# Two transformer blocks on one core: the output product by halves, its norm weights as a row, and chunk 3 of each such product one token later

## The chip, the cores and the metric

The kernel runs on one core of one Trainium2 chip. The time is that of one execution on the device, in microseconds (us); less is better. Three runs of the kernel before gave 1738.46, 1740.90 and 1743.47, median 1740.9.

## What is computed

Two transformer blocks on 512 tokens of 1024 features, in float32. The change touches four places of the same kind: a product of all tokens with a weight matrix, an RMS norm of its rows, a sum onto the residual h, and the RMS norm of h that begins the next stage. Cut to these:

```
mixed = concat(rmsnorm(y_conv), rmsnorm(y_att))
h = h + rmsnorm(mixed @ w_out, norm_mix_post)        # "out", then "hx"
hn = rmsnorm(h, norm_x_pre)
qx = hn @ w_q_x                                      # "qx"
kx, vx = split(rmsnorm(mem, norm_mem) @ w_kv_x)      # "kx", "vx": from mem, not from h
ox = softmax(qx kx^T / 16) vx
h = h + rmsnorm(ox @ w_o_x, norm_x_post)             # "ox", then "hf"
hn = rmsnorm(h, norm_ffn_pre)
h = h + rmsnorm((silu(g) * up) @ w_down, norm_ffn_post)   # "down0..2", then "h2"
# second block: ... h = h + merged @ w_out_2 ("out2", then "h4"), and a last MLP onto h
rmsnorm(x, g) = x / sqrt(mean(x^2) + eps) * g        # over the 1024 features of a token
```

## The kernel before, in words

**Products in three parts.** Each float32 operand is split into a high part (cast to float32r) and a low part (the rest); a product is high x high, high x low and low x high, all summed in one PSUM bank. Weights come in chunks of 1 MB: SyncE (SP) loads a chunk into one of three raw buffers, ScalarE casts it to w_high (`high`, L930, the cast at L945), GpSimd (POOL) subtracts it into w_low in four parts of 512 columns (`low_parts`, L783, at L801). w_high and w_low have a ring of two; a chunk in HOMES (L59) has buffers of its own in the arena (L372) and waits for no chunk of the ring. A raw buffer is loaded anew when the chunk three before has its low part; SP goes through the plan (make_plan) in order, so whatever waits in `before` (L627) holds the loads behind it.

**Groups by rows.** `rows` (L126) makes a group like out, vx, ox, down and out2: two halves of 512 output columns, each in two chunks of (mostly) 512 rows of the weights. So chunks 0 and 1 give the first half, chunks 2 and 3 the second, each for four tiles of 128 tokens (for vx two tiles, of mem). `product` (L2292) of one chunk and one token tile is 12 matmuls of 512 columns, eight with w_high (L2325, L2326), then four with w_low (L2329), each of which waits for its part of w_low. I write 2.1 for chunk 2 and token tile 1. down2 has 6 row blocks, so its chunks 1 and 3 are half as long. Groups by columns (gu, qx, up) are T mode, L2334 to L2338; where a stage does them in pieces between others (L2246 to L2248), a piece is three matmuls.

**Norm and turn.** The next product needs h normed, scaled and transposed. `stat` (L947) is the sum of squares and the root on ScalarE. `xn` (L1493) is the scaling on VectorE into stage: for the phases in NATURAL (L60) by the root and a row of norm weights that was loaded into all partitions (L1503), for the others by the root alone (L1508). `turn` (L2225, the transposes at L2222) lets TensorE turn the eight blocks of one token tile into two banks. For the phases in DIRECT ScalarE then casts the bank to xT_high (L965) and VectorE subtracts to xT_low (`lows`, L1510, at L1517). For the others VectorE first multiplies by the norm weights as a column (L1534), ScalarE casts that (L968) and VectorE subtracts (L1541).

**The four places before.** ox, down2 and out2 are done by `by_token` (L2250) on TensorE: chunks 0 and 1 for all tokens, then 2.0, 3.0, 2.1, 3.1, 2.2, turn 0, 3.2, 2.3, turn 1, 3.3, and turns 2 and 3 among the first products of the next stage (`first_tiles`, L2264). On ScalarE and VectorE, ox and down2 have `post_halves` (L1127, L1848): the first half's squares are summed and its norm weights multiplied in while TensorE does the second half; then, for each token, square, root, sum onto h (L1880), sum of squares of h, scaling.

out is different. TensorE does its four chunks one after another for all tokens, then vx's four chunks for two tiles each, with turn 0 to turn 2 of hx behind chunks 1 to 3 of vx, and turn 3 behind it (L2532 to L2547). ScalarE (`post`, L1168) copies every tile to ynat, takes the sum of squares over 1024 columns, and VectorE (`post`, L1790, and `staggered`, L1800) scales, adds to h and scales again, by the column way. Then the first 16 pieces of qx (chunk 0), which need all tokens of hx (`low_all`), and the cross-attention, which does the other pieces between its own steps.

## Time and profile before

| | |
|---|---|
| median of three runs | 1740.9 us |
| the profiled execution: time, span | 1742.11 us, 1740.4 us |
| busy TensorE, GpSimd, ScalarE, VectorE | 96%, 42%, 38%, 36% |
| mean granted clock of TensorE | 0.986 |
| out chunk 0 begins; chunk 2; vx; qx; cross-attention | 304.3; 330.8; 352.5; 393.2; 407.0 us |
| down2's and out2's turn 0 | 914.2; 1368.6 us |

The span is that of one execution, taken by the hardware profiler; the time is measured around it. A line of the timeline gives the start, the length, the engine, the line of the kernel, the operation with what it writes and reads, and in brackets how long the engine had been idle and whose work released it. "PEclk" is the share of TensorE's full clock that was granted. Matmuls are pipelined, so each record overlaps the next: one of 512 columns is 0.39 us long and starts 0.23 us after the one before. In records that merge several (x4), the length is of the group.

### The profile page before, as it was taken

The numbers are of one execution on the slowest core, as the hardware profiler recorded it, in microseconds if no ns is written. First come the engines' busy times: TensorE is split into PE (matmuls) and PEld (weight loads), VectorE is DVE, ScalarE is ACT, GpSimd is POOL, SyncE is SP. The second block draws the span as 40 slices with busy tenths as digits, with TensorE's granted clock in tenths as the row PEclk, the third lists the DMA queues.
The fourth block names the chain that finished last, engine by engine and source line by source line (L and its number), as shares of the span: only waits on it lengthen the run. The fifth ranks groups of instructions, "written<-read, shape, count | busy, mean of one in ns | idle before, by whom it ended". The sixth has DMA issues, their size and how long they took to land. (4 is left out here: it accounts for less than half of the span.)

```text
span 1740.4 us, 22686 instructions
## 1 busy us (share of the span) xinstructions
PE 1666.9 (96%) x8699; PEld 1325.8 (76%) x8699; DVE 632.5 (36%) x1169; ACT 666.8 (38%) x1005; POOL 733.4 (42%) x639
## 2 busy tenths in 40 slices
PE   7989899979999999999998999999999999999999
PEld 5767668757668888878877787767778888888887
DVE  6432765272324111101137534454556331213131
ACT  4223567363344233231235534443554431313140
POOL 5223334463143443454443544323454354444443
PEclk9999899999999999999999999999999999999999
DMA  5243202232131433343231234222254323232321
GB/s 175 75 145 83 72 26 74 85 132 70 41 96 43 127 97 97 97 143 92 71 108 49 93 101 140 77 83 84 74 200 151 97 73 97 97 97 97 97 98 49
DMA packets 152876, 165.55 MB, mean 95 GB/s; under 512 B 11981, under 2 KB 114496, under 8 KB 152768
## 3 DMA queue, kind: packets, MB, share of 16 engines
q1 hardware_dynamic: 145152, 150.69, 27.1%
q10 hardware_dynamic: 7616, 13.41, 2.2%
q8 instruction: 69, 1.13, 0.3%
q14 instruction: 39, 0.32, 0.1%
HBM read 155.17 MB, written 9.30 MB: 94 GB/s over the span
## 5 line engine op out<-in xcount | busy, mean ns | idle before, releaser
L801 POOL TENSOR_TENSOR w_low<-raw,w_high 128x512 fp32r<-128x512 f32 x505 | 671.5, 1362 | 888.2 <-ACT w_high L945 887.8
L945 ACT CAST w_high<-raw 128x2048 fp32r<-128x2048 f32 (+1 forms) x128 | 241.2, 1884 | 255.6 <-PE bank L2329 242.3
L2334 PE MATMUL bank<-xT_high,w_high 128*128 128x512 f32 (+1 forms) x672 | 249.2, 376 | 0.0
L2335 PE MATMUL bank<-xT_low,w_high 128*128 128x512 f32 (+1 forms) x672 | 248.8, 375 | 0.0
L2325 PE MATMUL bank<-w_high,hid_high 128*128 128x512 f32 x432 | 172.0, 398 | 0.3 <-ACT w_high L945 0.3
L2326 PE MATMUL bank<-w_high,hid_low 128*128 128x512 f32 x432 | 171.8, 398 | 0.0
L2338 PE MATMUL bank<-xT_high,w_low 128*128 128x512 f32 (+1 forms) x672 | 156.6, 375 | 0.7 <-POOL w_low L801 0.7
L2246 PE MATMUL bank<-xT_high,w_high 128*128 128x512 f32 (+1 forms) x360 | 152.4, 423 | 3.7 <-DVE xT_low L1541 3.2
L2335 PEld LDWEIGHTS bank<-xT_low,w_high 128*128 128x128 f32 x672 | 127.3, 189 | 22.4
L2334 PEld LDWEIGHTS bank<-xT_high,w_high 128*128 128x128 f32 x672 | 127.2, 189 | 22.4
L2248 PE MATMUL bank<-xT_high,w_low 128*128 128x512 f32 (+1 forms) x360 | 142.6, 396 | 0.0
L2247 PE MATMUL bank<-xT_low,w_high 128*128 128x512 f32 (+1 forms) x360 | 142.0, 394 | 0.0
L2338 PEld LDWEIGHTS bank<-xT_high,w_low 128*128 128x128 f32 x672 | 121.0, 189 | 23.6 <-POOL w_low L801 1.3
L2329 PE MATMUL bank<-w_low,hid_high 128*128 128x512 f32 x432 | 120.4, 399 | 1.7 <-POOL w_low L801 1.7
L2325 PE MATMUL bank<-w_high,xT_high 128*128 128x512 f32 x256 | 102.3, 400 | 3.5 <-DVE xT_low L1541 3.5
L2326 PE MATMUL bank<-w_high,xT_low 128*128 128x512 f32 x256 | 100.8, 394 | 0.0
L2329 PEld LDWEIGHTS bank<-w_low,hid_high 128*128 128x128 f32 x432 | 82.0, 190 | 22.3 <-POOL w_low L801 2.4
L2325 PEld LDWEIGHTS bank<-w_high,hid_high 128*128 128x128 f32 x432 | 81.6, 189 | 20.4 <-ACT w_high L945 0.7
L2326 PEld LDWEIGHTS bank<-w_high,hid_low 128*128 128x128 f32 x432 | 81.7, 189 | 19.8
L2198 DVE TENSOR_TENSOR h<-h,bank 128x512 f32<-128x512 f32 x40 | 27.5, 688 | 172.9 <-PE bank L2329 172.8
L2246 PEld LDWEIGHTS bank<-xT_high,w_high 128*128 128x128 f32 (+1 forms) x360 | 67.9, 189 | 27.8 <-issue 9.0
L1902 DVE TENSOR_TENSOR qbuf<-silu,bank 128x512 f32<-128x512 f32 x22 | 15.1, 688 | 187.8 <-PE bank L2338 187.8
(427 smaller groups left out, 2542.9 us busy)
## 6 DMA issues: line engine op xcount, KB each, us to landing
raw<-in_w_in SPq DMA_DIRECT2D x33, 1024.0 KB, 5.0
raw<-in_w_down SPq DMA_DIRECT2D x26, 1024.0 KB, 5.0
raw<-in_w_gate_up SPq DMA_DIRECT2D x44, 512.0 KB, 5.0
raw<-in_w_up SPq DMA_DIRECT2D x16, 1024.0 KB, 5.2
raw<-in_w_kv_x SPq DMA_DIRECT2D x8, 1024.0 KB, 5.2
raw<-in_w_out SPq DMA_DIRECT2D x8, 1024.0 KB, 5.0
gate_dram<-qbuf ACTq DMA_DIRECT2D x20, 256.0 KB, 2.0
sg<-gate_dram ACTq DMA_DIRECT2D x6, 768.0 KB, 5.3
```

Source lines behind the costliest of these rows:

```text
L801: ins = pool.tensor_tensor(low[:, cs], full[:, cs], high[:, cs], ALU.subtract)
L945: own.tell(act.copy(split_slot(c, wh), split_slot(c, raw)), wh_done)
L2198: own.tell(dve.tensor_tensor(y, y, src[:, :], ALU.add), dense_v)
L2246: pe.matmul(ps, ah, bh, start=first, stop=False)
L2247: pe.matmul(ps, ah, bl, start=False, stop=False)
L2248: return pe.matmul(ps, al, bh, start=False, stop=last)
L2325: pe.matmul(ps[:, :], xh[:, k, js], ch[:, q, :], start=first and q == 0, stop=False)
L2326: pe.matmul(ps[:, :], xl[:, k, js], ch[:, q, :], start=False, stop=False)
L2329: mm = pe.matmul(ps[:, :], xh[:, k, js], cl[:, q, :], start=False, stop=last and q == len(ks) - 1)
L2334: pe.matmul(ps[:, t0:t1], ch[:, k, cs], xh[:, k, t0:t1], start=q == 0, stop=False)
L2335: pe.matmul(ps[:, t0:t1], ch[:, k, cs], xl[:, k, t0:t1], start=False, stop=False)
L2338: mm = pe.matmul(ps[:, t0:t1], cl[:, k, cs], xh[:, k, t0:t1], start=False, stop=q == len(ks) - 1)
```

## The change

- Chunks 2 and 3 of out are done by token, as in by_token, with turns 0 and 1 of hx inside; vx follows, product by product, with turn 2 behind its first and turn 3 behind its third; the other five stand between turn 3 and qx.
- out and hx take the way of ox and hf: post_halves on ScalarE and VectorE, norm_x_pre as a row (hx in NATURAL), no copy of the tiles to ynat by ScalarE, no column product. The old `post` and `staggered` go.
- vx's first chunk gets a home of its own, at 16448 and 24640 of the arena, where the attention's probabilities were.
- SP loads norm_mix_post and norm_x_pre ahead of out's chunk 3; before, norm_mix_post stood ahead of vx. norm_ffn_pre goes into the same row as norm_x_pre, so its load waits for hx's last scaling.
- ScalarE casts vx's chunk 1 ahead of the last square of out and chunk 2 ahead of hx's last copies; its copies of vx's tiles come after all of hx.
- In all four places (out, ox, down2, out2) the order is now 2.0, 2.1, 3.0, 3.1, 2.2, turn 0, and on as before.

post_halves of VectorE is moved up unchanged; it is shown once, where it is added.

```diff
@@ -56,8 +56,8 @@
 
 HEAD_GAINS = (("g_na_q_2", ND), ("g_na_k_2", ND), ("g_mem_q_2", MD), ("g_mem_k_2", MD))
 GAIN_LOADS = sum(P // d for _, d in HEAD_GAINS)
-HOMES = {"gu0": 0, "if": 0, "up0": 1}
-NATURAL = ("hf", "h2", "h4")
+HOMES = {"gu0": 0, "if": 0, "up0": 1, "vx": 2}
+NATURAL = ("hx", "hf", "h2", "h4")
 DIRECT = NATURAL + ("hm", "hna")
 
 
@@ -164,7 +164,7 @@
     p.columns("xin", w_in, [1024, 1280], readers="V")
     p.columns("kx", a["w_kv_x"], [0, 256, 512, 768])
     p.use(0, 1, 2, 3)
-    p.rows("out", a["w_out"], 0, 2, 4)
+    p.rows("out", a["w_out"], 0, 2, 4, readers="V")
     p.use(0, 1)
     p.rows("vx", a["w_kv_x"], 1024, 2, 2, readers="X")
     p.columns("qx", a["w_q_x"], [0, 256, 512, 768])
@@ -370,7 +370,8 @@
         rtmp = at("rtmp", o, [P, 2, S])
         gnat = [at("gain_natural", 49216, [P, D]), shared[:, 0:D]]
         homes = [(at("home_high_0", 61504, [P, CW], F32R), at("home_low_0", 69696, [P, CW], F32R)),
-                 (at("home_high_1", 8192, [P, CW], F32R), at("home_low_1", 24576, [P, CW], F32R))]
+                 (at("home_high_1", 8192, [P, CW], F32R), at("home_low_1", 24576, [P, CW], F32R)),
+                 (at("home_high_2", 16448, [P, CW], F32R), at("home_low_2", 24640, [P, CW], F32R))]
         hidh, hidl = at("hid_high", 0, [P, 8, S], F32R), at("hid_low", 16384, [P, 8, S], F32R)
 
...
@@ -629,8 +630,8 @@
                 "kv": lambda: (vector_loads(), position_loads()),
                 "kcvc": lambda: small_loads(),
                 "kx": lambda: (late_mem(), bias_windows()),
-                "vx": lambda: post_gain("norm_mix_post", o_taken, 2 * ST),
-                "ox": lambda: (post_gain("norm_x_post", h_ready, 4), natural_gain(0, "norm_ffn_pre", pv_done, 2 * ST * PER_GROUP)),
+                "ox": lambda: (post_gain("norm_x_post", h_ready, 4),
+                               natural_gain(0, "norm_ffn_pre", xn_ready, ntile["hx", 3] + 1)),
                 "down0": lambda: second_memory(),
                 "gu2": lambda: (post_gain("norm_ffn_post", h_ready, 8),
                                 natural_gain(0, "g_mix_2", xn_ready, ntile["hf", 3] + 1)),
@@ -710,6 +711,9 @@
                         x_load(j)
                 if c is c.group.chunks[0] and c.group.name in before:
                     before[c.group.name]()
+                if c is G["out"].chunks[3]:
+                    post_gain("norm_mix_post", o_taken, 2 * ST)
+                    natural_gain(0, "norm_x_pre", pv_done, 2 * ST * PER_GROUP)
                 if c.group.name == "gate2":
                     i = c.group.chunks.index(c)
                     for hd in beside.get(i, ()):
@@ -889,8 +893,7 @@
             low_parts(len(plan.chunks))
 
         STATS = [("x", j) for j in range(4)] + [("mem", j) for j in range(2)] + [("att", j) for j in ATT_ORDER]
-        STATS += [("yo", 0), ("yo", 1), ("hx", 0), ("yo", 2), ("hx", 1), ("yo", 3), ("hx", 2), ("hx", 3)]
-        for ph, nx in (("yx", "hf"), ("yf", "h2")):
+        for ph, nx in (("yo", "hx"), ("yx", "hf"), ("yf", "h2")):
             if ph == "yf":
                 STATS += [("mem2", j) for j in range(2)]
             STATS += [k for j in range(ST) for k in ((ph, j), (nx, j))]
@@ -899,7 +902,7 @@
         SOURCES = {"x": h, "hx": h, "hf": h, "h2": h, "h4": h, "mem": mem_nat, "mem2": mem_nat2, "att": yatt}
         TURNED = {"mem": (memTh, memTl), "mem2": (mem2Th, mem2Tl), "hm": (hmTh, hmTl), "hna": (hmTh, hmTl)}
 
-        FREE = {"hx": "out", "hf": "qx", "h2": "gu2", "h4": "gate2"}
+        FREE = {"hf": "qx", "h2": "gu2", "h4": "gate2"}
 
         def turned(i, b, low):
 
@@ -936,6 +939,8 @@
                     act.wait_ge(raw_in[c.n % RAW], loaded[c.n])
                     if c.before is not None:
                         used(act, c.before)
+                    if c.group.name == "vx" and c.home is not None:
+                        act.wait_ge(pv_done, 2 * ST * PER_GROUP)
                     if c.group.name == "gu0" and c.home is not None:
                         act.wait_ge(x_out, 2 * XH)
                     if c.group.name == "up0" and c.home is not None:
@@ -1124,7 +1129,7 @@
             for j in ATT_ORDER:
                 hi(ntile["att", j])
 
-            def post_halves(group, yname, hname, src_ready, following):
+            def post_halves(group, yname, hname, src_ready, following, later=None):
 
                 g = G[group]
                 summed = yname == "yf"
@@ -1159,38 +1164,13 @@
                     if j:
                         hi(ntile[hname, j - 1])
                     residual_stat(hname, j, src_ready)
+                if later:
+                    high(later.n)
                 hi(ntile[hname, 3])
 
             def residual_stat(hname, j, src_ready):
                 act.wait_ge(h_ready, src_ready + j + 1)
                 stat((hname, j), h[:, j, :], D)
...
-            def post(group, yname, hname, src_ready, filler=None):
...
             def vx_out(j):
 
@@ -1202,7 +1182,9 @@
                         act.wait_ge(dense_done, n + 1)
                         own.tell(act.copy(vx[:, t % 2, 512 * (t // 2):512 * (t // 2) + 512], tile_bank(n)[:, :]),
                                  vx_taken)
-            post("out", "yo", "hx", 0, vx_out)
+            post_halves("out", "yo", "hx", 0, G["vx"].chunks[0], G["vx"].chunks[2])
+            for j in range(4):
+                vx_out(j)
             pieces_out(pieces("qx")[0:16])
 
 
@@ -1787,30 +1769,45 @@
             ql("att", third)
             ql("att", last)
 
-            def post(yname, j, gains):
-
-                k = STATS.index((yname, j))
-                dve.wait_ge(rms_done, k + 1)
+            def post_halves(group, yname, hname, gains, squared):
+                g = G[group]
+                summed = yname == "yf"
                 dve.wait_ge(gpost_in, 16 * gains)
-                own.link(dve.reciprocal(rms[:, k:k + 1], rms[:, k:k + 1]))
-                own.link(dve.scalar_tensor_tensor(out=ynat[:, j, :], in0=ynat[:, j, :], scalar=rms[:, k:k + 1],
-                                                  in1=gpost[:, :], op0=ALU.mult, op1=ALU.mult))
-                own.tell(dve.tensor_tensor(h[:, j, :], h[:, j, :], ynat[:, j, :], ALU.add), h_ready)
-
-            def staggered(name, j):
-
-                if j:
-                    xn(name, j - 1, D)
-                if j >= 2:
-                    ql(name, j - 2)
-                if j == 3:
-                    xn(name, 3, D)
-                    ql(name, 2)
-                    ql(name, 3)
-
-            for j in range(ST):
-                post("yo", j, 1)
-                staggered("hx", j)
+
...
+                def take(t):
+                    half, j = t // 4, t % 4
+                    cs = slice(512 * half, 512 * half + 512)
+                    y = ynat[:, j, cs]
+                    if summed:
+                        own.tell(dve.tensor_tensor(y, y, tile_in(group, t)[:, :], ALU.add), dense_v)
+
+                def scale(t):
+                    half, j = t // 4, t % 4
+                    cs = slice(512 * half, 512 * half + 512)
+                    y = ynat[:, j, cs]
+                    dve.wait_ge(y_sq, squared + t + 1)
+                    if summed:
+                        own.link(dve.tensor_tensor(y, y, gpost[:, cs], ALU.mult))
+                    else:
+                        own.tell(dve.tensor_tensor(y, tile_in(group, t)[:, :], gpost[:, cs], ALU.mult), dense_v)
+
+                for t in range(ST):
+                    take(t)
+                for t in range(ST):
+                    scale(t)
+                for j in range(ST):
+                    k = STATS.index((yname, j))
+                    take(4 + j)
+                    scale(4 + j)
+                    dve.wait_ge(rms_done, k + 1)
+                    own.link(dve.reciprocal(rms[:, k:k + 1], rms[:, k:k + 1]))
+                    own.tell(dve.scalar_tensor_tensor(out=h[:, j, :], in0=ynat[:, j, :], scalar=rms[:, k:k + 1],
+                                                      in1=h[:, j, :], op0=ALU.mult, op1=ALU.add), h_ready)
+                    if j:
+                        lows(hname, j - 1)
+                    xn(hname, j, D)
+                lows(hname, 3)
+            post_halves("out", "yo", "hx", 1, 0)
 
 
...
-            post_halves("ox", "yx", "hf", 2, 0)
+            post_halves("ox", "yx", "hf", 2, 8)
...
@@ -1916,7 +1875,7 @@
                     src = tile_in(f"down{s}", t)
                     y = ynat[:, j, 512 * half:512 * half + 512]
                     own.tell(dve.tensor_tensor(y, y, src[:, :], ALU.add), dense_v)
-            post_halves("down2", "yf", "h2", 3, 8)
+            post_halves("down2", "yf", "h2", 3, 16)
 
 
             R = gate_rows
@@ -2255,9 +2214,16 @@
                         pe.wait_ge(low, base + c[i].kts[-1] + 1)
                     for k in range(first if i == 0 else 0, ST):
                         product(c[i], k, xh, xl)
-                for j in range(ST):
+                last_half(c, xh, xl, phase)
+
+            def last_half(c, xh, xl, phase):
+
+                product(c[2], 0, xh, xl)
+                for j in range(1, ST):
                     product(c[2], j, xh, xl)
-                    if j >= 2:
+                    if j == 1:
+                        product(c[3], 0, xh, xl)
+                    else:
                         turn(phase, j - 2)
                     product(c[3], j, xh, xl)
 
@@ -2529,21 +2495,21 @@
                     turn("mem", s - MEM_STEP)
 
             pe.wait_ge(conv_lo, 4)
-            for i, c in enumerate(G["out"].chunks):
-                if i == 1:
-                    low_all("att")
-                for k in range(ST):
-                    if i == 0 and k >= 2:
-                        pe.wait_ge(o_taken, 2 * ST - 3 + k)
-                    product(c, k, xTh, xTl)
-                    if i == 0:
-                        turn("att", ATT_ORDER[k])
-            for i, c in enumerate(G["vx"].chunks):
-                for k in range(2):
-                    product(c, k, memTh, memTl)
-                if i:
-                    turn("hx", i - 1)
-            turn("hx", 3)
+            c = G["out"].chunks
+            for k in range(ST):
+                if k >= 2:
+                    pe.wait_ge(o_taken, 2 * ST - 3 + k)
+                product(c[0], k, xTh, xTl)
+                turn("att", ATT_ORDER[k])
+            low_all("att")
+            for k in range(ST):
+                product(c[1], k, xTh, xTl)
+            last_half(c, xTh, xTl, "hx")
+            tiles = [(c, k) for c in G["vx"].chunks for k in range(2)]
+            for i, (c, k) in enumerate(tiles):
+                product(c, k, memTh, memTl)
+                if i in (0, 2):
+                    turn("hx", 2 + i // 2)
             low_all("hx")
             x_pieces(pieces("qx")[0:16])
 
```

## Rows read from the trace of the kernel before

**Rows 1.** Page, part 1: busy us (share of the span) x instructions

```profile
PE 1666.9 (96%) x8699; PEld 1325.8 (76%) x8699; DVE 632.5 (36%) x1169; ACT 666.8 (38%) x1005; POOL 733.4 (42%) x639
```

**Rows 2.** Timeline, PE, 352 to 394: start us, us, engine, line, out<-in, [idle before <-releaser]

```profile
352.54 0.39 PE L2325 MATMUL bank<-w_high,memT_high 128*128 128x512 f32 x1
...
367.79 1.10 PE L2329 MATMUL bank<-w_low,memT_high 128*128 128x512 f32 x4
...
370.61 1.09 PE L2329 MATMUL bank<-w_low,memT_high 128*128 128x512 f32 x4
...
377.62 0.50 PE L2329 MATMUL bank<-w_low,memT_high 128*128 128x512 f32 x1 [1.05 <-POOL w_low L801]
...
382.48 1.29 PE L2222 MATMUL bank<-ident,stage 128*128 128x128 f32 x8 [1.55 <-DVE qbuf L1534]
...
388.04 1.94 PE L2222 MATMUL bank<-ident,stage 128*128 128x128 f32 x8 [4.27 <-DVE qbuf L1534]
...
393.17 0.79 PE L2246 MATMUL bank<-xT_high,w_high 128*128 128x512 f32 x1 [3.19 <-DVE xT_low L1541]
```

**Rows 3.** Timeline, PE, ACT and DVE, token 0 in ox

```profile
511.19 0.50 PE L2329 MATMUL bank<-w_low,oxT_high 128*128 128x512 f32 x1 [0.73 <-POOL w_low L801]
...
512.49 1.28 ACT L1157 ACT_TABLE_LOAD   x1
...
514.38 1.72 DVE L1880 SCALAR_TENSOR_TENSOR h<-ynat,rms,h 128x1024 f32<-128x1024 f32 x1
...
517.97 1.28 DVE L1503 SCALAR_TENSOR_TENSOR stage<-h,rms,gain_natural 128x1024 f32<-128x1024 f32 x1
...
519.90 1.04 PE L2222 MATMUL bank<-ident,stage 128*128 128x128 f32 x8
```

**Rows 4.** Windows: us, busy of PE PEld DVE ACT POOL, PEclk, DMA share, GB/s

```profile
387.00:397.00 10.00, 5.77 (x17) 4.62 (x18) 5.70 (x9) 4.37 (x5) 2.62 (x3) 0.50 0.59 206
...
398.00:406.00 8.00, 8.00 (x37) 6.41 (x35) 0.00 (x0) 0.60 (x1) 1.39 (x2) 1.00 0.38 131
```

**Rows 5.** Timeline, PE, chunks 2 and 3 of out

```profile
330.78 0.39 PE L2325 MATMUL bank<-w_high,xT_high 128*128 128x512 f32 x1
...
341.66 0.39 PE L2325 MATMUL bank<-w_high,xT_high 128*128 128x512 f32 x1
```

**Rows 6.** Timeline, POOL, low part of out's chunk 3

```profile
333.70 5.03 POOL L801 TENSOR_TENSOR w_low<-raw,w_high 128x512 fp32r<-128x512 f32 x4 [7.66 <-ACT w_high L945]
```

**Rows 7.** Timeline, SP; DMA issues by line (KB each, median us to landing)

```profile
305.99 0.35 SPq L667 DMA_DIRECT2D share<-in_norm_mix_post  x1
...
gain_natural<-in_norm_ffn_pre SPq DMA_DIRECT2D x1, 512.0 KB, 6.9
```

**Rows 8.** Timeline, PE, POOL and DVE, out2: w_low products of 2.0 and 2.1, token 0

```profile
1354.33 1.10 PE L2329 MATMUL bank<-w_low,yT_high 128*128 128x512 f32 x4
...
1362.06 1.09 PE L2329 MATMUL bank<-w_low,yT_high 128*128 128x512 f32 x4
...
1359.88 5.06 POOL L801 TENSOR_TENSOR home_low<-raw,home_high 128x512 fp32r<-128x512 f32 x4
...
1363.88 2.15 DVE L1503 SCALAR_TENSOR_TENSOR stage<-h,rms,share 128x1024 f32<-128x1024 f32 x1
```

**Rows 9.** Timeline, PE, the pieces of qx before the attention

```profile
397.38 0.39 PE L2247 MATMUL bank<-xT_low,w_high 128*128 128x512 f32 x1
...
405.80 0.39 PE L2248 MATMUL bank<-xT_high,w_low 128*128 128x512 f32 x1
```

**Rows 10.** Timeline, PE, ox: w_low products of 2.0 and 2.1

```profile
504.63 1.10 PE L2329 MATMUL bank<-w_low,oxT_high 128*128 128x512 f32 x4
...
513.38 1.10 PE L2329 MATMUL bank<-w_low,oxT_high 128*128 128x512 f32 x4
```

**Rows 11.** Timeline, ACT and PE, down2

```profile
906.75 0.30 ACT L945 CAST home_high<-raw 128x128 fp32r<-128x128 f32 x1 [5.71 <-POOL home_low L792]
...
914.21 1.09 PE L2222 MATMUL bank<-ident,stage 128*128 128x128 f32 x8 [0.66 <-DVE stage L1503]
```

85 lines of the change are left out of this document (30 added, 55 removed).

## The prediction

> **What bounds the kernel now.** I read the page first: TensorE is busy 96% of the span, the next engine 42% [rows 1]. A microsecond counts only if TensorE waits, or runs at its lower clock, in it. The chain of waits is TensorE's own work, so the second view is TensorE's order of time, in the stretches that the diff touches. From the first product of vx at 352.54 to the first piece of qx at 393.17 it takes 40.6 us [rows 2]. Its work there is eight products at 2.82 (370.61 less 367.79) and four turns at about 0.94 (1.04 busy in ox [rows 3], of which a tenth overlaps the next product), 26.3 us. The other 14.3 us are waits. The largest are 1.55, 4.27 and 3.19 us on VectorE, which scales, turns over and splits the rows of h while TensorE has nothing left; smaller ones, as 1.05 us at 377.62, are for w_low [rows 2]. The windows show what follows: the granted clock is 0.50 from 387 to 397, the lower of two levels (1.2 and 2.4 GHz), after the long waits, and 1.00 again from 398 [rows 4].
>
> **Part A, order of the output product and of vx.** Chunks 0 and 1 of out stay. Chunk 2 begins at 330.78, and four products from there take 10.88, so 2.72 each [rows 5]. The new order is 2.0, 2.1, 3.0, 3.1, 2.2, turn 0, 3.2, 2.3, turn 1, 3.3 (chunk.token). Product 3.0 begins at 336.2. Its w_low on GpSimd now runs from 333.70 for 5.03 us [rows 6]; the cast ahead of it moves by some 0.4, because ScalarE squares and shifts token 3 where it copied it. The fourth part is then there at 339.1 and wanted at 338.7: 0.4 lost, and 3.0 ends at 339.35. Two products on, turn 0 could start at 344.8.
>
> Token 0's chain decides whether it may. ox has the same code already. There the last w_low matmul of 3.0 starts at 511.19 and the scaled row is in stage at 517.97 + 1.28 = 519.25, 8.06 us, of which 1.28 is a table load [rows 3]. The out stage comes out of a square root, and the squares between need no other table, so I take 6.8 us (with the load: 8.1, the upper bound). From 339.12 that is 345.9, and 0.3 more where GpSimd splits the first vx chunk beside it: 346.1. So the price of the new chain is a wait of 1.3 us, where the 14.3 us were. Then come four turns (3.8), the three products left (8.2) and eight of vx (22.6): qx can begin at 380.6 instead of 393.17. **Gain 12.6.**
>
> What could wait in between: turn 1 comes 6.4 us after turn 0 (two products and a turn); the chain from token to token takes about 5 us by the operations of ox, as 1.28 + 0.69 + 1.28 + 1.28 on VectorE, with ScalarE's sum of squares inside. Turns 2 and 3 now stand behind one vx product and two more. By the ox durations token 3 is in stage some 1.5 us before turn 3 wants it, at 365.4. Five vx products lie behind turn 3, 14 us, and cover its two copies and two subtractions (about 3 us); low_all costs nothing. Were that cover gone, the 3 us would be paid. ScalarE's casts in its queue: vx chunk 0 goes into a home of its own, ahead of the squares; chunk 1 waits for 2.3 (352.5) and stands ahead of square 7; chunk 2 ahead of the last copies; each then has 5 to 6 us of GpSimd, and by this count its parts come as they are wanted, within half a microsecond, for 362.7, 369.3 and 374.9. Next late is w_low of vx chunk 3: a part 1 us late costs 1 us.
>
> The queues: SP issues the first gain row at 305.99 [rows 7], which now stands with norm_x_pre ahead of out's chunk 3. A row of 512 KB landed after 6.9 us in a busy moment [rows 7]. Three loads one behind the other at that price end at 326.7; the cast, some 2 us ahead of the split at 333.70 [rows 6], wants chunk 3 at 332. The next load has until 334, when ScalarE has cast chunk 3. So nothing, and from there on a microsecond for each late. SP's new wait ahead of ox, for token 3's scaled row (about 364 by this count), holds up ox's first load alone, whose slot comes free only when qx's second chunk is split, after 380. GpSimd's queue gets nothing new.
>
> VectorE: per token 1.28 + 1.28 us plus one 0.69 before turn, in place of two full-width operations, a tensor_scalar and two gain products; ScalarE drops eight copies. Off the path but for token 0, counted above.
>
> Of VectorE the rows say: the same scaling of 1024 columns takes 1.28 us in ox at 517.97 and 2.15 us in out2 at 1363.88, most of it beside a split on GpSimd that runs from 1359.88 for 5.06 us; the addition to h takes 1.72 at 514.38 [rows 3, 8]. In out GpSimd splits from about 339 to 344, beside the addition and perhaps the start of the scaling: hence my 0.3. The Trainium skill (Advanced Engine Details and Errata, Mode Summary) says that GpSimd and VectorE share VectorE's second port and block each other. It speaks against this change, which brings GpSimd's split of vx beside token 0, and it is what rival 2 goes by.
>
> **Part B, the clock in qx.** The ten intervals from 393.17 to 397.38 take 4.21 us; the 37 from there to 405.80 take 0.2276 each [rows 2, 9]. At that pace the ten are 2.28. The waits that precede the fall are gone, so **gain 1.9**. Bounds: 0, if the clock falls all the same, and 2.8 with the turn at 388.04 (1.94 against 1.04 [rows 2, 3]), which is already in the 14.3.
>
> **Part C, ox.** The w_low groups of 2.0 and 2.1 start 8.75 us apart [rows 10], two products are 5.58: 3.17 are lost in 3.0, on the weights of chunk 3. The new order takes 2.1 first and loses nearly nothing, but the last w_low part comes no sooner, so 3.0 ends where it did and its chain, too. Turn 0, at 519.90, was not waiting; it now waits for 519.25. **Gain 0.6**, not 3.2, with a wait of 2.2 us.
>
> **Part D, down2.** Turn 0 waits already, until 914.21, for a chain that begins with ScalarE's cast of the gate weights, held by GpSimd until 906.75 [rows 11]. Products 2.1 and 3.0 change places ahead of that, so **gain 0**; the idle time becomes one stretch of some 5 us before turn 0. Bounds: +0.2 and -1.5, if the clock falls there.
>
> **Part E, out2.** The groups are 7.73 apart against 5.60 [rows 8]: 2.13 lost. 3.0 ends at 1360.2 and the row is in stage at 1366.03, 5.8 later [rows 8]. Now it ends at 1354.33 + 0.93 + 5.6 = 1360.87, and stage at 1366.7; turn 0 was at 1368.6. **Gain 1.9.**
>
> **Sum**: 12.6 + 1.9 + 0.6 + 0 + 1.9 = 17.0. What follows each stage is in TensorE's order and moves up whole. The profiled execution has a span of 1740.4 and a time of 1742.1, 1.2 over the median of three, 1740.9. On it: 1725.1; on the median **1723.9**.
>
> **Rivals.**
> 1. *The waits come back with the clock.* After each new wait before turn 0 (1.3, 2.2, 5 us) the clock falls. One such fall cost 1.9 us in qx and 0.9 in the turn. For: a wait of 4.27 was followed by one [rows 2, 4]. Against: the waits of 1.05 and 1.55 before it weren't: the turn at 382.48 took 1.29 us, not 1.94 [rows 2]. Falls in out and ox, 2.8 each, give 1729.5.
> The Trainium skill (TensorE: Matmul & The Clock Gate, What's actually happening) says that an idle stretch puts the array at half rate and sustained work brings it back; the trace agrees for 387 to 397, and for down2 it would make this rival sure, though there VectorE's chain covers most of it.
> 2. *The shared port.* Addition and scaling of token 0 both at 2.15, 4.3 us for 3.0, of which 0.3 is counted: 1.0 more. And the splits of vx, slowed in turn, late for two chunks by the 1.05 us of 377.62 [rows 2]: 3.1 us less, 1727.0.
> 3. *More than counted*: token 0's chain short enough to spare the waits in out (1.3) and in ox (2.2): 1720.4.
> 4. *Slower.* The lower clock, in all four products: a stretch at half rate costs half its length. The longest seen is 10 us [rows 4], 5 us if it is all work. Four such behind the four turns 0 take 20 of the 17: 1743.9. It decides from 34 us at the lower level on. Against: the one wait of that size in the rows is in vx, and it goes.
> 5. *A new wait in vx.* That the change doesn't do what it says is hardly open; the order is written out. But if vx's last products wait for ScalarE's copies of vx tile 0 (they stand behind the copies of turn 3), 1 to 3 us come back: 1726.
>
> **How the numbers follow.** Forecast with its small errors, 0.62; rival 1 0.13; 2 0.08; 3 0.07; 4 0.03; 5 0.07. The likeliest gives 1723.9. The range leaves out rival 4 and the far ends: 1719.5 to 1730. A measurement of this kernel can tell 0.3%, 5 us, from no change: all but rival 4 are faster by more. Rival 4 is split between same and slower, with something for what I overlooked: faster 0.95, same 0.02, slower 0.03.
>
> **What would show it.** Right: qx's first piece at 380 to 381, 12 to 13 us earlier than now, no wait on xT_low before it, matmuls of 0.39 from its start; turn 0 waits 1 to 2 us for stage in out, about 2 in ox, 5 in down2, near 0 in out2; turn 0 of ox moves by less than 1 us against the start of ox. Wrong: turn 0 of out after 348, w_low waits in vx over 1 us, a granted clock of 0.5 between 346 and 381, or ox and out2 as long as before.

## The result, and the profile after

The changed kernel takes **1725.14 us** (median of four runs, 1721.92 to 1727.71) where the kernel before takes 1740.29 in the same set (four runs, 1738.46 to 1743.47). The ratio is 0.9911, 95% interval 0.9900 to 0.9923: 15.2 us less, where 17.0 were forecast. The profiled execution took 1727.71 us, its span is 1726.0, at a mean granted clock of 0.987.

Page, part 1: busy us (share of the span) x instructions, against [rows 1].

```profile
PE 1662.4 (96%) x8699; PEld 1326.5 (77%) x8699; DVE 621.0 (36%) x1165; ACT 663.8 (38%) x1009; POOL 729.8 (42%) x639
```

The span is 14.4 us shorter. TensorE has as many instructions as before and is busy 4.5 us less, so 9.9 us of the gain are idle time. Where they come from shows in the order of time only.

Timeline, PE, from chunk 1 of out to the cross-attention (start us, us, engine, line, operation, [idle before <-releaser]); turns are L2181, first matmuls of w_low L2295, the first piece of qx L2205, the scores of the attention L2527. It answers to [rows 2, 5].

```profile
320.29 0.50 PE L2291 MATMUL bank<-w_high,xT_high 128*128 128x512 f32 x1 [2.35 <-DVE xT_low L1523]
...
339.76 0.50 PE L2295 MATMUL bank<-w_low,xT_high 128*128 128x512 f32 x1 [0.35 <-POOL w_low L805]
...
346.96 1.09 PE L2181 MATMUL bank<-ident,stage 128*128 128x128 f32 x8 [1.24 <-DVE stage L1485]
...
353.36 1.03 PE L2181 MATMUL bank<-ident,stage 128*128 128x128 f32 x8
359.73 1.03 PE L2181 MATMUL bank<-ident,stage 128*128 128x128 f32 x8
366.16 1.04 PE L2181 MATMUL bank<-ident,stage 128*128 128x128 f32 x8
...
381.07 0.39 PE L2205 MATMUL bank<-xT_high,w_high 128*128 128x512 f32 x1
...
392.96 1.10 PE L2527 MATMUL bank<-kxT,qxT 128*128 128x256 f32 x4 [0.84 <-ACT qxT L1044]
```

The brackets are what to read. Before, turns 2 and 3 and the first piece of qx waited 1.55, 4.27 and 3.19 us for VectorE [rows 2]; now 0.35 us for w_low in product 3.0 and 1.24 us ahead of turn 0 are all that is left, and turns 1 to 3, eight products of vx and qx follow without a gap. It is closer than it looks: token 3's scaled row is in stage at 365.97 and its turn starts at 366.16. The granted clock agrees (windows; us, busy of PE PEld DVE ACT POOL, PEclk, DMA share, GB/s), against [rows 4]:

```profile
371.00:381.00 10.00, 10.00 (x44) 8.06 (x43) 0.00 (x0) 4.12 (x3) 8.32 (x8) 1.00 0.53 172
381.00:393.00 12.00, 11.16 (x51) 8.92 (x49) 0.00 (x0) 3.69 (x4) 6.94 (x6) 1.00 0.81 280
```

The other three places, by the same view: ox, down2 and out2.

```profile
472.19 0.50 PE L2291 MATMUL bank<-w_high,oxT_high 128*128 128x512 f32 x1 [1.53 <-DVE oxT_low L1841]
...
505.61 1.29 PE L2181 MATMUL bank<-ident,stage 128*128 128x128 f32 x8 [2.05 <-DVE stage L1485]
513.70 1.03 PE L2181 MATMUL bank<-ident,stage 128*128 128x128 f32 x8
520.24 1.03 PE L2181 MATMUL bank<-ident,stage 128*128 128x128 f32 x8
526.34 1.53 PE L2181 MATMUL bank<-ident,stage 128*128 128x128 f32 x8 [2.19 <-DVE stage L1485]
...
901.67 1.97 PE L2181 MATMUL bank<-ident,stage 128*128 128x128 f32 x8 [4.99 <-DVE stage L1485]
...
1354.40 1.04 PE L2181 MATMUL bank<-ident,stage 128*128 128x128 f32 x8
```

The two spans, cut at places that both kernels have (all from the two timelines of PE). "The first product of ox" is here and below the first behind the attention, at 472.19; two others stand inside the attention. The column on the right is what the change was forecast to do between the two places.

| from, to | before | after | difference | forecast |
|---|---|---|---|---|
| start to out chunk 1 | 319.77 | 320.29 | +0.5 | 0 |
| to the attention (A, B) | 87.26 | 72.67 | -14.6 | -14.5 |
| to the first product of ox | 78.91 | 79.23 | +0.3 | 0 |
| to down2's turn 0 (C) | 428.27 | 429.48 | +1.2 | -0.6 |
| to out2's turn 0 (D, E) | 454.38 | 452.73 | -1.7 | -1.9 |
| to the end | 371.81 | 371.60 | -0.2 | 0 |

One step is off by more than half a microsecond: ox. Turn 0 moved as forecast (33.96 us behind the first product of ox before, 33.42 now, with a wait of 2.05 where 2.2 was forecast). But turn 1 follows 8.09 us later instead of 6.45. The clock tells why (windows of the changed kernel, PE alone, same columns without the other engines):

```profile
472.20:505.60 33.40, 31.19 (x132) 1.00 0.36 98
505.60:514.00 8.40, 8.39 (x35) 0.80 0.40 111
514.00:526.00 12.00, 10.15 (x75) 1.00 0.01 2
526.00:532.00 6.00, 5.66 (x35) 0.72 0.62 175
```

Behind the wait of 2.05 us the products run partly at the lower level (1.2 of 2.4 GHz), 1.6 us longer in all. That is rival 1, in one of its places. So three questions were open: which part of the change the 14.6 us need, whether the loss in ox is the clock's, and whether it can be had back.

### The profile page after: what moved, and what is told of

It is laid out like the page before. It is cut to its first block and busy times, and to the rows that moved or that the text cites. A ratio compares the mean times of both kernels' runs of the same rounds, so it can differ in the third digit from the quotient of the medians.

```text
span 1726.0 us, 22688 instructions
## 1 busy us (share of the span) xinstructions
PE 1662.4 (96%) x8699; PEld 1326.5 (77%) x8699; DVE 621.0 (36%) x1165; ACT 663.8 (38%) x1009; POOL 729.8 (42%) x639
## 5 line engine op out<-in xcount | busy, mean ns | idle before, releaser
L805 POOL TENSOR_TENSOR w_low<-raw,w_high 128x512 fp32r<-128x512 f32 x501 | 662.0, 1352 | 877.0 <-ACT w_high L950 876.6
L950 ACT CAST w_high<-raw 128x2048 fp32r<-128x2048 f32 x127 | 239.3, 1884 | 244.1 <-PE bank L2295 230.7
L2205 PE MATMUL bank<-xT_high,w_high 128*128 128x512 f32 (+1 forms) x360 | 152.3, 423 | 0.7 <-ACT qbuf L1317 0.4
L2295 PE MATMUL bank<-w_low,hid_high 128*128 128x512 f32 x432 | 119.6, 397 | 0.0
L2295 PEld LDWEIGHTS bank<-w_low,hid_high 128*128 128x128 f32 x432 | 81.7, 189 | 20.0 <-POOL w_low L805 0.2
L2205 PEld LDWEIGHTS bank<-xT_high,w_high 128*128 128x128 f32 (+1 forms) x360 | 67.8, 188 | 24.5 <-issue 9.0
```

Source lines behind the costliest of these rows:

```text
L805: ins = pool.tensor_tensor(low[:, cs], full[:, cs], high[:, cs], ALU.subtract)
L950: own.tell(act.copy(split_slot(c, wh), split_slot(c, raw)), wh_done)
L2205: pe.matmul(ps, ah, bh, start=first, stop=False)
L2295: mm = pe.matmul(ps[:, :], xh[:, k, js], cl[:, q, :], start=False, stop=last and q == len(ks) - 1)
```

## The experiments

The kernel before was timed beside the experiments in three sets, each on another chip: 1741.02 us (median) in that of experiments 1, 2 and 4, 1738.7 in that of 6, 7 and 8, 1739.73 in that of 3, 9 and the second timing of the changed kernel. Ratios are to the kernel before of the same set. The changed kernel has 0.9911 in its own set and 0.9915 in the last; across sets only ratios are compared, and 0.001 is 1.7 us.

**1. The new order alone, and all but it.** In the first, the kernel before with only this edit (so out keeps its old way):

```diff
-                for j in range(ST):
+                product(c[2], 0, xh, xl)
+                for j in range(1, ST):
                     product(c[2], j, xh, xl)
-                    if j >= 2:
+                    if j == 1:
+                        product(c[3], 0, xh, xl)
+                    else:
                         turn(phase, j - 2)
```

> The kernel before with one edit: chunk 3 meets token 0 behind chunk 2's token 1 in ox, down2 and out2; out, vx and hx as before. My theory (the weights' wait of 3.0 goes, but token 0's chain takes its place in ox and brings half rate there): against the kernel before, turn 0 of ox moves up 0.5 and turn 1 of ox back by about 1.1, down2 stays, with one wait of 5 us before turn 0, out2 gains 2.1; in sum 0.5 to 1.5 us faster, not measurable. Rival (the chain has slack, the weights' waits of 3.2 and 2.1 are saved whole): 5 us faster. Rival (half rate behind every new wait): 1 to 3 us slower.

Measured: 1740.92 us, ratio 1.0002 (0.9993 to 1.0011). In the second, the changed kernel with the old order in ox, down2 and out2:

> The changed kernel with the old order in ox, down2 and out2; out keeps the new one. Theory: all of the gain of the output stage stays, so 14.5 us faster than before and within 1 us of the changed kernel: ox 1.1 better than changed at turn 1, out2 2.1 worse. Rival (the order is worth 5 us): 5 us behind the changed kernel.

Measured: 1727.24 us, ratio 0.9923 (0.9909 to 0.9937). So the gain is that of out: 13.4 of the 15 us are there without the new order elsewhere, and the rest is inside the intervals. The order in the other three places is worth nothing that can be measured. The profile of the first says why: turn 0 of ox stands 33.42 us behind the first product, 0.5 less than before, after a wait of 2.03, and turn 1 at 41.52 instead of 40.41; from down2's turn 0 to out2's it takes 452.30 us instead of 454.38. What out2 gains (2.1), ox gives back in part (1.1). What ox gains in weights it pays in clock; its mean granted clock is 0.982 to 0.987 over its runs, where the kernel before in the same set has 0.984 to 0.987.

The six runs of the second fall into two groups: three of 1724.2 to 1724.6 us at a mean clock of 0.989 to 0.990, three of 1729.9 to 1730.9 at 0.986 to 0.987. That was the first sign that the spread of this kernel is the clock's. (The second kernel is 2.1 us above the changed one by either measure; expected was 1 us at most.)

**2. Without the home of vx's chunk 0.** The changed kernel; ScalarE casts the ring's chunks in the ring's order, since chunk 0 must now wait for the ring buffer of out's chunk 2 (`ringed` is true where the chunk that follows has no home):

```diff
-HOMES = {"gu0": 0, "if": 0, "up0": 1, "vx": 2}
+HOMES = {"gu0": 0, "if": 0, "up0": 1}
...
-                    high(c.n + 1)
+                    high(min(c.n + 1, g.chunks[-1].n) if ringed else c.n + 1)
...
-                        high(following.n + 1)
+                        high(following.n if ringed else following.n + 1)
...
-                    high(later.n)
+                    high(later.n - 1 if ringed else later.n)
```

> The changed kernel without a home for vx's first chunk: its cast waits for chunk 2's last use and stands where chunk 1's stood, the other casts one place later. Theory: the home spares TensorE the cast at the start of vx, 1.6 us, and about as much at vx's second chunk: 3 us slower than the changed kernel, qx begins at 384. Rival (cover everywhere, the home is worth nothing): as the changed kernel. Rival (weights bound vx: every chunk late by cast and split, 7 us for 5.6 of work): 8 us slower.

Measured: 1737.97 us, ratio 0.9983 (0.9975 to 0.9992): 12 to 13 us of the gain are gone, four times what was expected, and more than the second rival's 8. Timeline of PE:

```profile
356.51 0.50 PE L2292 MATMUL bank<-w_high,memT_high 128*128 128x512 f32 x1 [1.62 <-ACT w_high L950]
...
361.39 0.51 PE L2296 MATMUL bank<-w_low,memT_high 128*128 128x512 f32 x1 [1.71 <-POOL w_low L805]
362.62 0.79 PE L2296 MATMUL bank<-w_low,memT_high 128*128 128x512 f32 x1 [0.73 <-POOL w_low L805]
363.21 1.91 PE L2182 MATMUL bank<-ident,stage 128*128 128x128 f32 x8
369.31 0.50 PE L2292 MATMUL bank<-w_high,memT_high 128*128 128x512 f32 x1 [0.91 <-ACT w_high L950]
```

and of GpSimd, in this kernel and then in the changed one:

```profile
332.84 5.03 POOL L805 TENSOR_TENSOR w_low<-raw,w_high 128x512 fp32r<-128x512 f32 x4 [9.79 <-ACT w_high L950]
356.60 5.97 POOL L805 TENSOR_TENSOR w_low<-raw,w_high 128x512 fp32r<-128x512 f32 x4 [18.74 <-ACT w_high L950]
```

```profile
334.67 5.04 POOL L805 TENSOR_TENSOR w_low<-raw,w_high 128x512 fp32r<-128x512 f32 x4 [8.12 <-ACT w_high L950]
339.78 6.03 POOL L805 TENSOR_TENSOR home_low<-raw,home_high 128x512 fp32r<-128x512 f32 x4
358.86 6.02 POOL L805 TENSOR_TENSOR w_low<-raw,w_high 128x512 fp32r<-128x512 f32 x4 [13.04 <-ACT w_high L950]
```

With the home GpSimd splits vx's chunk 0 straight behind out's chunk 3, in time in which it has nothing else. Without it GpSimd is idle for 18.74 us, and the four chunks of vx then come at its pace and ScalarE's, one product at a time. The waits of old are gone in both; without the home new ones stand in their place, all but one (0.76 us for ScalarE's copy of vx) for weights. The attention starts 87.64 us behind chunk 1 of out, where it was 87.26 in the kernel before; 1.6 of them are a fall of the clock behind chunk 1 (experiment 5), and a second, from 362.6, ends in a wait for weights.

**3. The home alone**, in the kernel before (the entry in HOMES, its two buffers, ScalarE's wait for the attention's probabilities):

> The kernel before with one part of the change alone: chunk 0 of vx has a home of its own instead of a ring buffer; out product, token order and column of weights for hx as before. Theory now held (the buffers, more than the order of the products, were what held TensorE behind the out product: without the home the whole change was worth 3 us, with it 15): the waits for w_low at 377 to 393 us of before (1.05, 1.55, 4.27 and 3.19 us) fall to 5 us or less in sum, the attention starts at most 82 us behind chunk 1 of out (before 87.3), and the time is 1732 to 1735 us. Rival: the home is worth its 12 us only together with the early casts of the halves, since in the kernel before the cast of vx chunk 0 stands in ScalarE's queue behind the work on the tokens whether its buffer is free or not: the waits stay within 1 us in sum, the attention starts 86 us or more behind chunk 1, and the time is 1738 to 1741 us.

Measured: 1740.85 us (ten runs, 1735.26 to 1745.2), ratio 1.0005 (0.9992 to 1.0019). The rival holds. PE and, below, GpSimd:

```profile
376.95 0.51 PE L2332 MATMUL bank<-w_low,memT_high 128*128 128x512 f32 x1 [1.06 <-POOL w_low L802]
381.80 1.29 PE L2225 MATMUL bank<-ident,stage 128*128 128x128 f32 x8 [1.54 <-DVE qbuf L1537]
387.36 1.94 PE L2225 MATMUL bank<-ident,stage 128*128 128x128 f32 x8 [4.27 <-DVE qbuf L1537]
392.49 0.80 PE L2249 MATMUL bank<-xT_high,w_high 128*128 128x512 f32 x1 [3.19 <-DVE xT_low L1544]
```

```profile
339.55 5.04 POOL L802 TENSOR_TENSOR home_low<-raw,home_high 128x512 fp32r<-128x512 f32 x4
```

The four waits are those of [rows 2], within 0.01 us. The chunk is split 3.5 us earlier against chunk 1 of out than before (20.7 behind it, not 24.2), and nobody waits for it. The home and the rest of the change are each worth next to nothing (0 and 3 us) and together 15: before, VectorE's chain was last and the weights had slack; in the changed kernel turn 0 stands 26.7 us behind chunk 1 instead of 45.3, and the weights are last, unless they have a place to be early in. The rest of the change is three things in out: the order by token, the work by halves, and the row. The row is taken out in experiment 4; order and halves were never parted, so their shares are open.

**4. hx by the column way.** The changed kernel with hx out of NATURAL: scaled by its root alone, multiplied by the norm weights as a column after the turn; norm_x_pre is not loaded as a row.

```diff
-NATURAL = ("hx", "hf", "h2", "h4")
+NATURAL = ("hf", "h2", "h4")
...
-                        lows(hname, j - 1)
+                        (ql if hname == "hx" else lows)(hname, j - 1)
```

> The changed kernel with hx scaled by the column of norm_x_pre again (scaling by the root alone, a product of two banks by the column per token, casts from that), all else as changed. Theory: turns 0 of hx up to 0.5 us earlier, since the plain scaling is shorter, and 0.9 us more of VectorE per token, which the two products between turns cover: turns 1 to 3 wait 1 us at most in sum, qx begins within 1 us of the changed kernel; the gain came from the order and the halves, not from the row. Rival (the row of weights is what takes the chain off the path): turns 1 to 3 wait 1 us or more each, 3 to 5 us slower.

Measured: 1730.25 us, ratio 0.9940 (0.9927 to 0.9953), about 5 us more than the changed kernel; the expectation fell, its rival held in the time (3 to 5 us; of the turns only one waits more than 1 us). In its profile turns 0 to 3 wait 0.70, 0.40, 0.35 and 1.84 us, and w_low of a vx product 0.64, where the changed kernel has one wait of 1.24. Counted without the fall behind chunk 1, turn 0 comes 0.5 us sooner (the scaling is cheaper) and turn 3 stands 23.3 us behind it instead of 19.2: all four turns wait for VectorE's scaled row. I put it down to the column products, two for each token, which are too much for VectorE between turns. I had counted them as hidden, by their sum. Behind the wait of 1.84 the granted clock is 0.79 from 369.8 to 378.0: another fall.

**5. Is it the clock?** Every profile without fills (experiment 8) has the same wait of 2.35 us ahead of out's chunk 1, and the same products behind it. The distance from there to the last w_low matmuls of 3.0 takes two values, and so does turn 0 to turn 1 in ox:

| | out: chunk 1 to 3.0's w_low | ox: first product to turn 1 |
|---|---|---|
| the clock stays | 19.5 us: changed kernel, turn 0 later (6) | 39.9 us: column way (4) |
| the clock falls | 21.1 us: all but the order (1), no home (2), column way (4), vx ahead (7), filled in ox (9), changed kernel again | 41.5 us: changed kernel, order alone (1), no home (2), vx ahead (7), changed kernel again |

In windows of PE, the changed kernel and then its profile in the last set (the clock is the third figure from the right):

```profile
320.30:339.80 19.50, 19.15 (x84) 1.00 0.17 55
```

```profile
318.10:339.20 21.10, 20.73 (x83) 0.92 0.15 51
```

Left out are the profiles in which the edit touches the place: the old order, or fills. (Where out has its old order, the granted clock behind the same 2.35 us stays at 1.00 in two profiles and falls in the home alone: 7 falls in 11. Ahead of ox's turn 3 ten profiles have a wait of 2.2 to 2.4 us, and nine a fall behind it.) The waits are equal to 0.05 us, so what follows a wait of 2.0 to 2.35 us is not settled by its length: in most executions the lower level, in some not, and each fall costs 1.6 us. The changed kernel was run again for this:

> The changed kernel, nothing edited, beside the others on the same chip. Theory (half clock after a wait of 2.0 to 2.35 us comes in some executions and not in others, at 1.6 us a time): its runs lie in steps between 1721.5 and 1729 us, the later ones at a lower mean granted clock (0.986 to 0.987 at the top, 0.989 to 0.990 at the bottom), median 1724 to 1726. Rival (the spread is not the clock's): the mean clock is the same within 0.001 in the fastest and the slowest run.

Measured: 1725.24 us (1724.32 to 1728.21), ratio 0.9915 (0.9901 to 0.9930), the result again. The slowest run has a mean clock of 0.986, the fastest 0.989; 0.003 of 1725 us is 5 us, for 3.9 us of difference. The theory holds within the rounding of the clock; with four runs, steps can't be told. The profile of this run has the same two falls in ox (turn 0 of 1.83 us, turn 3 of 1.97).

**6. Turn 0 of hf one product later**, in ox: 2.0 2.1 3.0 3.1 2.2 3.2 T0 2.3 T1 3.3.

> The changed kernel with turn 0 of ox one product later: 2.0, 2.1, 3.0, 3.1, 2.2, 3.2, turn 0, 2.3, turn 1, 3.3. Theory (token 0's chain is late by 2 us there and by nothing else): no wait before turn 0, about 1.3 us before turn 1, which comes some 39 us after the first product of ox (41.5 in the changed kernel's trace, with half rate in it), and the end of chunk 3 two us earlier; 1 to 2.5 us faster than the changed kernel. Rival (the chain is bound from token to token, not by token 0): turn 1 and all behind it stay where they are, no gain.

Measured: 1722.62 us, ratio 0.9906 (0.9893 to 0.9920). The wait is now 1.24 us before turn 1, with no fall behind it; turn 3 waits 2.40 us, with one (1.97 us long). Turn 3 stands 52.05 us behind the first product of ox, 2.1 sooner than in the changed kernel: 1.6 for the fall that went, 0.5 for the order. In the time, 0.9 us by the ratios, it can't be told from the changed kernel; the profile carries this experiment.

**7. A product of vx ahead of turn 0**, to fill the 1.24 us in out. The second product moves ahead of turn 2, the third and fourth ahead of turn 3, and ScalarE copies vx's first two tiles ahead of hx's last casts:

> The changed kernel with vx's products spread further: the first ahead of turn 0 of hx, the second between chunk 3's last product and turn 2, the third and fourth ahead of turn 3; ScalarE copies vx's first two tiles ahead of hx's last casts. Theory: the 1.24 us before turn 0 of hx go, nothing takes their place, and the first piece of qx comes 1.2 us earlier against out's chunk 1; 1.2 us faster. Rival (vx's first product so early waits for its w_low, or its bank): the wait only moves, no gain.

Measured: 1729.69 us, ratio 0.9944 (0.9931 to 0.9958), 5 to 6 us slower than the changed kernel by the ratios, not faster. The wait before turn 0 is gone, and two others are there:

```profile
366.64 0.51 PE L2297 MATMUL bank<-w_low,memT_high 128*128 128x512 f32 x1 [0.57 <-POOL w_low L805]
367.87 0.50 PE L2297 MATMUL bank<-w_low,memT_high 128*128 128x512 f32 x1 [0.72 <-POOL w_low L805]
```

Counted without the falls, the attention starts 73.4 us behind chunk 1 of out where it was 72.7: the slack of vx's chunk 1 was as small as the prediction said (parts that come as they are wanted), and the product taken from it is missed. That is 0.7 us, and it is there again in experiment 8 with all three edits (73.38 us, no fall). The copies that ScalarE does earlier may have a part in it; they were not tried alone. The profile also has the falls behind chunk 1 and in ox. The mean granted clock of its four runs is 0.985 to 0.987, that of the changed kernel's eight 0.986 to 0.989. So part of the rest is the clock's; why it is lower here stays open.

**8. Idle work in the waits.** If the clock falls because TensorE does nothing, work without use should hold it. Transposes of the identity into a bank that is free, 0.12 us each, put ahead of the waits:

```diff
+            def fill(n):
+
+                for _ in range(n):
+                    pe.transpose(bank[7][:, 0:P], ident[:, :], ident[:, :])
...
+                        if j == 2:
+                            fill({"hf": 14, "h2": 38}.get(phase, 0))
                         turn(phase, j - 2)
...
+                        if i == 1 and phase == "hf":
+                            fill(15)
...
+            fill(16)
             low_all("att")
```

and 20 ahead of the first tiles behind down2. The 16 stand ahead of out's chunk 1.

> The changed kernel with idle work of TensorE in five of its waits: transposes of a constant into a bank that nothing reads, 14 to 38 of them by the length of the wait (ahead of out's chunk 1; of turn 0 and turn 3 of ox; of turn 0 of down2; of the first tiles behind it). They compute nothing and take away no wait. Theory (the waits are followed, in some runs, by half rate that costs about 1.6 us each): the granted clock stays 1.00 behind all five, turn 1 of ox is 40 us after its first product in place of 41.5, and the time falls by 2 to 5 us, with less spread. Rival (the stretches at half rate come at their own times, whatever TensorE did): they stay, and the time is the same or worse. Rival (the work displaces real work): 1 to 3 us slower.

Measured: 1720.61 us (1720.30 to 1722.23), ratio 0.9897 (0.9882 to 0.9912), mean clock 0.992 to 0.993 in every run. In its profile 3.0's w_low is 19.5 us behind chunk 1, and turn 1 of ox 39.9 behind the first product. All three edits together (this, 6 and 7), with fills fitted to the new orders:

> The three edits together: vx's product ahead of turn 0, turn 0 of ox one product later, and the idle work in the waits that are left (nine transposes ahead of ox's turn 1 in place of fourteen ahead of its turn 0). Theory: the gains add, 4 to 8 us faster than the changed kernel, 1717 to 1721. Rival: they share their gain through the clock, and no more than the best of the three is left.

Measured: 1721.7 us (1719.61 to 1726.1), ratio 0.9901 (0.9887 to 0.9914). The gains don't add, the rival holds.

**9. Fills in ox alone, and fills with turn 0 later.** The first has only the 14 and the 15 transposes of ox:

> The changed kernel with idle transposes in ox alone: 14 before turn 0 of hf and 15 before turn 3. Theory (the 2.05 us wait before turn 0 brings half clock in most executions and costs 1.6 us when it does; the one before turn 3 is followed by the first tiles at either level): turn 1 stands 39.9 us behind the first product of ox instead of 41.5, turn 3 at most 52.6, and the median is 1 to 2 us under that of the unedited changed kernel in the same set, its spread smaller by about as much. Rival (all of the 4 us that the full set of fills gave was in down2 and in front of out chunk 1): within 0.5 us of the unedited kernel.

Measured: 1722.16 us (1720.32 to 1725.28), ratio 0.9897 (0.9882 to 0.9912), 3.1 us under the changed kernel in the same set, with intervals that overlap a little; the spread is no smaller (5.0 us, 3.9 in the changed kernel), against what was expected. The profile is plainer in ox:

```profile
472.60 0.50 PE L2300 MATMUL bank<-w_high,oxT_high 128*128 128x512 f32 x1 [1.53 <-DVE oxT_low L1841]
...
506.00 1.09 PE L2181 MATMUL bank<-ident,stage 128*128 128x128 f32 x8 [0.48 <-DVE stage L1485]
512.53 1.03 PE L2181 MATMUL bank<-ident,stage 128*128 128x128 f32 x8
519.08 1.03 PE L2181 MATMUL bank<-ident,stage 128*128 128x128 f32 x8
...
525.18 1.09 PE L2181 MATMUL bank<-ident,stage 128*128 128x128 f32 x8 [0.56 <-DVE stage L1485]
```

Turn 0 stands 33.40 us behind the first product, as in the changed kernel, so the data came no sooner; turn 1 at 39.93 and turn 3 at 52.58 instead of 41.51 and 54.15. And from turn 3 to down2's turn 0 it takes 373.74 us instead of 375.33: the second fall, which the kernel before had too (375.22). Two falls, 1.6 us each, 3.2 in all. For ox the theory holds. In the time the rival (within 0.5 us) is unlikely and not excluded. The profiled execution is the slowest of its four (1725.28 us) and no shorter than the profiled one of the changed kernel in this set (1725.34): chunk 1 of out begins 0.9 us later in it, and the attention has a stretch at the lower level (0.73 from 464 to 470) that the other lacks (1.00). Falls elsewhere can hide the gain of one place in one execution. Over all experiments, nine places in four profiles were filled where the unfilled wait is 2.0 to 2.4 us (out's chunk 1 three times, ox's turn 0 twice, its turn 3 four times), and no fall came behind any; unfilled, such waits were followed by one in 21 of 27 cases.

> The changed kernel with TensorE kept at work in its waits by idle transposes of the identity (in front of out chunk 1, of turns 0 and 1 and of the first tiles in down2, and in ox) and, in ox, with turn 0 of hf one product later: order 2.0 2.1 3.0 3.1 2.2 3.2 T0 2.3 T1 3.3, eight idle transposes before turn 1. Theory: in the first set the fills removed the falls of the clock (4 to 5 us) and the later turn 0 left a wait of 1.24 before turn 1 in place of 2.05 before turn 0, so that the two together give 0.5 to 1 us over the fills alone: 1719 to 1721 us, mean clock 0.993, all runs within 3 us. Rival (the later turn 0 only moves the wait on to turn 3, 2.40 in place of 2.19, and that stage's end is the same): 1720.5 to 1722.

Measured: 1722.93 us (1720.11 to 1724.28), ratio 0.9902 (0.9885 to 0.9918). From the first product of ox to down2's turn 0 its profile has 425.84 us, against 426.32 and 426.34 in the two with fills alone and 429.48 in the changed kernel; the later turn gives its 0.5 us there. In the medians it can't be seen: 1719 to 1721 was expected, and all runs within 3 us; they spread over 4.2. The fills of down2 gave nothing: from its turn 0 to out2's it takes 452.5 us in the kernel of experiment 8 and 452.7 in the changed one, though the clock stays at 1.00 where it was 0.50. What stands behind that turn waits for VectorE anyway.

All versions with fills or a later turn lie between 1720.6 and 1722.9 us, by the ratios 1 to 3 us under the changed kernel; their intervals overlap each other and, if only by a little, the changed kernel's too.

## Why the prediction was right

It said 1723.9 us, and 1719.5 to 1730; it came to 1725.1. Between the two profiles the span fell by 14.4 us, where the sum was 17.0; 1.8 of the 2.6 missing are in ox.

- **Part A** (12.6). Product 3.0's last w_low matmuls waited 0.35 us (0.4 forecast). Token 0's scaled row was ready at 345.28 + 1.62 = 346.90, 7.14 us behind them (7.0 forecast), with no table load among ScalarE's records there, as counted; turn 0 waited 1.24 (1.3). qx started at 381.07 instead of 393.17, and counted from chunk 1 of out that is 12.6 us. Turns 1 to 3 and w_low in vx had no wait: rival 5 and the half microsecond allowed for a chunk did not come. Two things in it were closer than said. It gave the home no price; experiment 2 shows that it covers 12 us. And it counted token 3's row 1.5 us ahead of turn 3; it was 0.2 us ahead, its addition having taken 2.02 us beside a split. There is luck in the match of the profiles: neither has the fall behind out's chunk 1 that 7 of 11 have, 1.6 us.
- **VectorE and GpSimd together.** Both records in the changed kernel:

```profile
342.06 1.35 DVE L1804 SCALAR_TENSOR_TENSOR h<-ynat,rms,h 128x1024 f32<-128x1024 f32 x1
...
345.28 1.62 DVE L1485 SCALAR_TENSOR_TENSOR stage<-h,rms,gain_natural 128x1024 f32<-128x1024 f32 x1
...
351.02 1.29 DVE L1485 SCALAR_TENSOR_TENSOR stage<-h,rms,gain_natural 128x1024 f32<-128x1024 f32 x1
```

  Token 0's scaling took 1.62 us beside the split that runs from 339.78 for 6.03 us, token 1's 1.29 without one: 0.33 us, where 0.3 were counted. The two operations took 2.97 us together; rival 2 had 4.3. The Trainium skill (Advanced Engine Details and Errata, Mode Summary) says that VectorE's second port is shared with GpSimd, and that GpSimd's instructions and VectorE's two-port ones interfere; the trace agrees that the engines slow each other, in both directions (the split takes 6.03 instead of 5.04 us). Whether this scaling is a two-port instruction, no run here shows.
- **Part B** (1.9). qx takes 11.9 us, was 13.9, at a clock of 1.00: 2.0.
- **Part C** (0.6) is the step that failed: ox lost 1.2 us. Turn 0 gained 0.54, and its wait was 2.05 of 2.2. Then the clock fell and took 1.6. The text had this mechanism as rival 1, at 2.8 us a fall (from the fall in qx) and in out and ox both; one came, at 1.6. The size was wrong because qx's fall was cut from 10 us at the lower level, behind two long waits (4.27 and 3.19 us); behind the waits of 2.0 to 2.4 us each fall here costs 1.6. The reason given against it, that waits of 1.05 and 1.55 us had not been followed by a fall, was true and said nothing of 2.2 us. The wait of 2.19 us before turn 3 of ox stood in the trace before. It and the fall behind it would have told, mechanism and size (timeline and windows of the kernel before): 3.0 x 0.25 + 3.1 x 0.31 = 1.7 us.

```profile
538.99 1.09 PE L2222 MATMUL bank<-ident,stage 128*128 128x128 f32 x8 [2.19 <-DVE stage L1503]
...
538.90:541.90 3.00, 2.91 (x20) 0.75 0.96 276
541.90:545.00 3.10, 3.10 (x21) 0.69 0.30 72
```

- **Part D** (0). As said: 4.99 us idle in one stretch before turn 0, which moved up by no more than the stage did. The clock falls with it (0.82 from 897 to 900, within the wait, 0.50 from 900 to 903, 0.55 to 906), hidden as counted. Out2's part came to 1.7 with what else moved by a few tenths, 1.9 forecast; turn 0 itself moved by 2.1 against the first group of 2.0.
- **Rival 4** (slower) needed 34 us at the lower level. Of the three new waits before a turn 0 (1.24, 2.05 and 4.99 us) two brought a fall: in ox it makes 8.4 us at a mean of 0.80, so 3.4 us at half, and in down2 6.8 us.
- The rest of the difference: 0.5 us in front of chunk 1 are not the change's; there the profiles of kernels with equal code lie between 316.3 and 320.3 us. The 0.3 in the attention probably are: from the first scores to the first product of ox inside the attention it takes 56.26 to 56.31 us in all eleven profiles with the changed out and 56.01 in the three with the old one. The prediction had 0 there; what lengthens it is open.

The Trainium skill (TensorE: Matmul & The Clock Gate, What's actually happening) says that an idle stretch puts the array at half rate. The trace agrees for 4.99 us. For waits of 2.0 to 2.35 us it is more changeable than that sentence: half rate followed the wait ahead of chunk 1 in 7 of 11 profiles and the one ahead of ox's turn 0 in five of six, and came in none in which fills had cut the wait to 0.6 us or less.

## What to carry to other kernels

Two edits that are worth 0 and 3 us alone can be worth 15 together: an order that brings a chain forward needs the weights to be early too, and a buffer is only worth what the order in front of it can use. So cost an edit at nothing only beside the cover that makes it so, and take the cover away once on the chip. And look at what the trace has behind TensorE's waits before you count a new one: here waits of 2.0 to 2.4 us cost their length and mostly 1.6 us on top. Some idle transposes in such a wait (their end before the data come) took that back where what follows is TensorE's own work; in down2, where VectorE's chain stands behind the wait, they gave nothing.

## What the runs showed of the hardware that was not expected

- The same wait, in the same code, is followed by the lower clock in some executions and not in others, and the step is always the same: 19.5 or 21.1 us, 39.9 or 41.5 us. This makes most of what the runs of this kernel differ by (three of 1724.2 to 1724.6 us and three of 1729.9 to 1730.9 in one experiment).
- The length of the turn's record does not tell it. Behind a wait, a turn of eight transposes is mostly 1.09 us long when the clock stays, and anything from 1.09 to 1.97 when it falls: in experiment 7 turn 0 of ox was 1.09 us long and turn 1 came 8.07 us behind it, so the fall began after the turn. And in the kernel before the turn at 382.48 was 1.29 us long at a granted clock of 1.00. The distance between two records, beside the granted clock, is the safer sign.
- VectorE and GpSimd side by side slow each other, by different amounts: in the changed kernel's out stage VectorE's operations of 128x1024 took 1.28 to 1.29 us alone and 1.35, 1.62 and 2.02 where a split overlapped them, and a split took 6.03 us instead of 5.04.
